# Experts' down blocks loaded four neighbouring rows to a partition, with the folds of gate and up reading every fourth column

## The reference

```python
def moe(h, router_w, router_b, w_gate, w_up, w_down):
    ...
    y = jnp.zeros_like(x)
    for e in range(N_EXPERTS):           # 16
        he = (jax.nn.silu(x @ w_gate[e]) * (x @ w_up[e])) @ w_down[e]
        y = y + w[:, e:e + 1] * he       # w: two experts chosen per token, the others 0
    return y.reshape(B, S, D)
```

## Time and profile before

| | |
|---|---|
| median of three runs | 1465.07 us (1457.2 to 1466.48) |
| span of the profiled execution | 1454.6 us |
| TensorE busy (matmul) | 1381.8 us, 95% |
| VectorE busy | 1126.3 us, 77% |
| ScalarE busy | 932.6 us, 64% |
| moved by DMA | 342.63 MB, mean 236 GB/s |
| expert stages | about 250 to 500 us and 707 to 960 us of the span |

### The profile page before, as it was taken

The page is one execution under the profiler, slowest core; times in us unless marked ns, Lnnn a source line. Parts: engine busy times, 40 slices in busy tenths (PEclk is TensorE's granted clock), DMA queues, the critical chain, the costliest instruction groups (busy, mean ns, idle before and its releaser), DMA issues.

```text
span 1454.6 us, 18747 instructions
## 1 busy us (share of the span) xinstructions
PE 1381.8 (95%) x7320; PEld 1146.0 (79%) x7320; DVE 1126.3 (77%) x1351; ACT 932.6 (64%) x1103; POOL 72.7 (5%) x78
## 2 busy tenths in 40 slices
PE   7999998999999899999899999979999998799998
PEld 5887886888888677666788888857788887699986
DVE  4765578999999777677999999976665557578872
ACT  4453545989898643584789898955545664356561
POOL 0000000000000000000000000000773000000000
PEclk9999998999999999998999999999999999899999
DMA  9644544999999934503699999956445434455550
GB/s 338 198 146 145 198 164 154 390 376 391 387 398 401 351 127 139 185 1 145 239 396 384 380 394 398 398 213 202 145 146 173 146 117 145 155 178 187 191 172 31
DMA packets 128477, 342.63 MB, mean 236 GB/s; under 512 B 10189, under 2 KB 17021, under 8 KB 111869
## 3 DMA queue, kind: packets, MB, share of 16 engines
q1 hardware_dynamic: 121632, 331.57, 62.8%
q10 hardware_dynamic: 6748, 9.77, 2.0%
HBM read 340.27 MB, written 1.05 MB: 235 GB/s over the span
## 4 chain that ended last, share of the span: by engine, by line
PE 78%; DVE 11%; ACT 5%; DMA 3%; issue 2%; ACTq 1%; DVEq 0%
PE PS L656 22%; PE PS L1287 17%; PE PS L503 9%; PE PS L581 6%; DVE wlo L468 5%; PE PS L559 5%; PE PS L1326 3%; ACT whi L462 3%; PE PS L1276 2%; DMA raw<-in_moe_w_gate 2%; PE PS L1364 2%; PE PS L1360 1%; PE PS L2023 1%; PE PS L1750 1%; PE PS L1776 1%
## 5 line engine op out<-in xcount | busy, mean ns | idle before, releaser
L468 DVE TENSOR_TENSOR wlo<-raw,whi 128x2048 fp32r<-128x2048 f32 x314 | 706.8, 2274 | 122.4 <-ACT whi L462 116.4
L462 ACT ACTIVATE whi<-raw 128x2048 fp32r<-128x2048 f32 x314 | 589.8, 1897 | 44.4 <-PE PS L559 17.3
L1287 PE MATMUL PS<-whi,xg 128*128 128x512 f32 x512 | 205.6, 402 | 0.0
L1287 PE MATMUL PS<-wlo,xg 128*128 128x512 f32 x512 | 200.5, 392 | 0.0
L656 PE MATMUL PS<-whi,th 128*128 128x512 f32 x480 | 193.5, 403 | 2.1 <-DVE wlo L468 2.0
L656 PE MATMUL PS<-whi,tl 128*128 128x512 f32 x480 | 190.2, 396 | 0.0
L656 PE MATMUL PS<-wlo,th 128*128 128x512 f32 x480 | 189.3, 394 | 0.0
L1287 PEld LDWEIGHTS PS<-whi,xg 128*128 128x128 f32 x512 | 96.4, 188 | 18.6
L1287 PEld LDWEIGHTS PS<-wlo,xg 128*128 128x128 f32 x512 | 96.3, 188 | 18.6
L656 PEld LDWEIGHTS PS<-whi,th 128*128 128x128 f32 x480 | 90.2, 188 | 25.1 <-issue 2.4
L656 PEld LDWEIGHTS PS<-whi,tl 128*128 128x128 f32 x480 | 90.1, 188 | 21.8
(11 more groups left out here) (404 smaller groups left out, 2264.9 us busy)
## 6 DMA issues: line engine op xcount, KB each, us to landing
raw<-in_moe_w_gate SPq DMA_DIRECT2D x64, 1024.0 KB, 7.5
raw<-in_moe_w_up SPq DMA_DIRECT2D x64, 1024.0 KB, 8.4
raw<-in_moe_w_down SPq DMA_DIRECT2D x64, 1024.0 KB, 7.7
raw<-in_w_in SPq DMA_DIRECT2D x32, 1024.0 KB, 5.2
raw<-in_ret_w_in SPq DMA_DIRECT2D x24, 1024.0 KB, 5.1
raw<-in_w_up SPq DMA_DIRECT2D x20, 1024.0 KB, 5.1
raw<-in_w_down SPq DMA_DIRECT2D x10, 1024.0 KB, 5.0
raw<-in_ret_w_out SPq DMA_DIRECT2D x8, 1024.0 KB, 5.0
```

The costliest lines, as they stand in the source:

```text
L462: nc.scalar.activation(s.whi[:, high, 0:kc, 0:wide], s.raw[:, slot, 0:kc, 0:wide], ACT.Copy).then_inc(s.hi_done, 1)
L468: nc.vector.tensor_tensor(s.wlo[:, slot, 0:kc, 0:wide], s.raw[:, slot, 0:kc, 0:wide], s.whi[:, high, 0:kc, 0:wide], ALU.subtract).then_inc ...
L1287: last = nc.tensor.matmul(PS[:, bank, :], stationary(c), w[:, q, c, :], start=(start and c == 0 and k == 0), stop=(stop and c == KC - 1 an ...
```

## The change

Two edits. `paired_sync` loads all six blocks of an expert by `"(p c) n -> p c n"`, so partition p of a down block holds rows 4p to 4p + 3 of w_down instead of rows p, p + 128, p + 256, p + 384. The hidden index of `hT` must then be laid out alike: the f-th fold takes columns f, f + 4, f + 8, ... of `gate_s` and `up_s` instead of 128 neighbouring ones.

```diff
         def paired_sync(sp, layer):
             b0 = moe_b0[layer]
             for n, (e, i) in enumerate(paired_order()):
-                load_block(sp, sweep_first, b0 + n, 0, [(expert_blocks(layer, e)[i], KC, 0, BW)], block_rows(i))
+                load_block(sp, sweep_first, b0 + n, 0, [(expert_blocks(layer, e)[i], KC, 0, BW)], "(p c) n -> p c n")
...
                 for f in range(4):
-                    nc.tensor.matmul(PS[:, fold_bank, f * SLOTS:(f + 1) * SLOTS], gate_s[:, f * P:(f + 1) * P], fold,
+                    nc.tensor.matmul(PS[:, fold_bank, f * SLOTS:(f + 1) * SLOTS], gate_s[:, :].rearrange("s (p c) -> s c p", c=KC)[:, f], fold,
                                      start=True, stop=True)
                 pe.wait_ge(s.up_out, v + 1)
                 for f in range(4):
                     m = nc.tensor.matmul(PS[:, fold_bank, SEQ + f * SLOTS:SEQ + (f + 1) * SLOTS],
-                                         up_s[:, f * P:(f + 1) * P], fold, start=True, stop=True)
+                                         up_s[:, :].rearrange("s (p c) -> s c p", c=KC)[:, f], fold, start=True, stop=True)
```

## The result

The changed kernel takes 1530.99 us (median of four runs, 1529.03 to 1531.91) against 1463.46 us for the kernel before beside it: ratio 1.047, 95% interval 1.0443 to 1.0497. It is slower, as forecast, but by 67.5 us instead of 50, and 3 us above the stated range.

What follows compares the result with a forecast made beforehand. TensorE was taken to bound the expert periods. Stepped fold loads add 29.4 us a layer, minus 4.45 and 4.8 us, together 49.7 us: 1504.3 us profiled, plus 10.5 to the median, 1515 us; range 1458 to 1528 us.

Steps and rivals of the forecast that it cites:

- What bounds the kernel: Expert periods: TensorE sets the pace from end to end, 16.03 us for a plain expert, with VectorE and DMA close behind.
- Edit 1 at nothing: Down blocks: new source order keeps 2 KB pieces and costs 0, with 0.2 us a block as upper bound.
- the rival of slower transfers: Down blocks take 3.5 instead of 2.75 us, +26 us over 32 experts, 1491 us; chance 0.05.
- that of 8 KB pieces: Down blocks arrive in 8 KB pieces and the step is free: at most 2 x 2.5 us back, 1460 us; chance 0.03.
- Edit 2, the load: Folds: each stepped weight load costs 0.115 us more, 0.225 us in all; 16 loads make 1.84 us an expert.
- The slack: Time TensorE loses to others in 15 expert periods, 4.45 and 4.8 us by layer; extra work is first taken from it.
- I let the extra work take all of it: Sum: waits are at most 1.2 us, under 1.84, so all slack is subtracted; if none were, 9.2 us more.
- TensorE's floor of 235.7 us: TensorE's own work in a layer's 15 periods: 10 x 16.03 us with a gather plus 5 x 15.08 us without.
- would another engine then set the pace?: Period grows to 17.87 us; VectorE has 15.8 us of work and transfers 15.3, so neither takes over.
- Signs named ahead: Profile after: fold pairs 0.2 us or more, folds 1.7 to 1.9 us, 15 periods about 263 us, DMA near 357 GB/s.

Runs made afterwards that it cites:

- wide folds: The changed kernel, but each stepped fold load is followed by a matmul moving the fold matrix twice, 128 columns instead of 64: 1514.45 us, ratio 1.0364.

## Why the prediction was right or wrong

**What bounds the kernel: right.** TensorE set the pace. The folds alone, which add nothing to VectorE, ScalarE or the queues, made the whole loss.

**Edit 1 at nothing: right**, and shown by itself (1.0002). The packets stayed at 2 KB, as read from the length of a row. So the rival of slower transfers is out, and that of 8 KB pieces too, since they did not arise. What such pieces would be worth is not settled by the run that made them.

**Edit 2, the load: right in mechanism, slightly low in size.** The 0.115 us was put between two other engines' prices. Measured are 0.120 to 0.123 us a pair, and 17.98 - 16.03 = 1.95 us an expert instead of 1.84: +3.5 us over 32 experts. The observation that no reader in the trace got through 16 bytes in less than 1.78 ns was the better guide: 128 x 1.78 = 0.228 us, where 0.231 to 0.234 was measured.

**The slack: too hopeful.** With the clock left out (wide folds) 15 periods take 266.05 us; 240.07 + 15 x 1.95 would be 269.3. So 3.3 us of slack were taken in a layer (3.5 in the second), not 4.45 and 4.8: about 2.5 us more time in both layers together. Here the step "I let the extra work take all of it" failed; which wait stayed was not tested. The slack itself was also read too small. TensorE's floor of 235.7 us counts a scatter in all 15 periods, but the first expert has no expert before it. The scatter's matmuls in the window of the first layer (us, PE, PEld, clock, DMA, GB/s) are 112, which is 14 times 8:

```profile
252.65:492.80 240.15, 28.34 (x112) 21.02 (x112) 1.00 1.01 391
```

The slot weights are missing once as well, in the last period. That is 1.86 + 0.34 = 2.2 us less floor, so 6.6 and 7.0 us were lost to others before. Had all of it been taken, as the prediction's rule says, the forecast would have been lower still.

**The clock: missing, and this is what put the time outside the range.** This is the step that failed. The prediction read off that TensorE has its full clock and gave the clock no term in the sum, without a reason why it should stay. The step that asked "would another engine then set the pace?" looked at engines only. It did not ask what TensorE does while it waits for a load: it moves 64 columns in 0.23 us instead of 0.11, for 3.7 us in a row. Measured: the clock fell to half behind the folds of fourteen of the 32 experts and added 15.1 us in the 30 periods. Without it, the run with wide folds is at 1514.45 us, inside the range. That this is so near the forecast of 1515 us is partly luck: it was measured beside a kernel before that took 1460.09 us, and so is 54 us more than that, not 50.

The sum in the profile's terms: 49.7 (forecast) + 3.5 (load) + 2.5 (slack) + 15.1 (clock) = 70.8 of 72.6 us. The last 1.8 us lie outside the 30 periods; 1.2 us of them are the slow scatter at the end of the second layer, and the rest was not followed. How much is put down to slack and how much to the clock depends on the run compared with: the changed kernel itself has almost no idle time left, but only because the clock took what the loads had not.

**Signs named ahead.** Longer fold loads, folds of 1.7 to 1.9 us in the chain, VectorE below 91% (238.41 / 273.64 = 87%) and unchanged packets all came; "15 periods in about 263 us" did not: of the gap between 273.64 and 263, 7.6 us are the clock.

## What to carry to other kernels

Here a stationary operand read at a step was paid by the 16 bytes it touches, about 1.8 ns each, once that exceeded the plain load. Put a turn where a reader gets it free, in this kernel ScalarE's read from PSUM. When a change thins out TensorE's work without leaving it idle, price the clock as well as the wait: here that was a fourth more (15.1 us) on top of the load's own cost (32 x 1.95 = 62.4 us). And before counting on larger DMA pieces, hold the block's width against the row's length.

## What the runs showed of the hardware

- TensorE's clock fell to half, in fourteen of 32 cases, behind 3.7 us of folds in which TensorE was never idle by the profile and moved 64 columns per 0.23 us. It fell too with straight loads that moved 64 and 2 columns in turns. In the runs whose folds were as long but moved 128 columns per 0.23 us, or 64 per 0.11 us, it was full in all 30 periods (1.00 in each layer).
- ScalarE reads PSUM at a step of four floats as fast as straight (592 and 588 ns for 128 x 512), but reads SBUF at that step or writes to it (1107 ns) at about half.
- Fold loads at steps two, three and four fit one figure, 1.80 to 1.86 ns for 16 bytes. The two stepped copies in the earlier trace rows, at 1.89 and 1.82 ns, and the moving side in the earlier trace rows, at 1.78 ns, are close to it. The Trainium skill, SBUF — State Buffer, section Door 1: The DMA port swizzle, names lines of 16 bytes and two accesses to each for full speed; the runs agree on both (two a line: 0.119 us, one a line: 0.231), and contradict its statement in the same place that a step of four floats is free.
- Source pieces of 2 KB that lie 4 KB or 512 KB from each other made no difference to this kernel: ratio 1.0002, and 7.8 against 7.7 us from issue to landing.
